# Hybrid decoder trunk on one core: output weights loaded into the place of their low halves, half of them split in the sample stage, loads by readiness, no products with the zero state

## The reference

```python
hn = rmsnorm(x, norm1)
xr, yr, qkv_raw, z, b_raw, a_raw = split(hn @ w_in)          # 512, 512, 1536, 512, 4, 4 columns
xc = causal_conv(xr) + b                                     # 4 taps, history from the state
h = rglru(xc, h0)                                            # a = exp(-8 sigmoid(xc Wa) softplus(-lam)); h = a h + u
out_rg = gelu(yr) * h
q, k, v = silu(causal_conv(qkv_raw)); q, k = l2norm(q) / sqrt(128), l2norm(k)
beta = sigmoid(b_raw); g = -exp(A_log) * softplus(a_raw + dt_bias)
# gated delta rule, per head, in chunks: triangular solve inside a chunk, a 128 x 128 state S between chunks
v_new = u - w @ S;  o = (q e^gc) @ S + qk @ v_new;  S = S * g_last + k_tail^T @ v_new
out_gdn = rmsnorm(o, gdn_norm_w) * silu(z)
x = x + concat(out_rg, out_gdn) @ w_out
hf = rmsnorm(x, norm2); x = x + (silu(hf @ w_gate) * (hf @ w_up)) @ w_down
y = rmsnorm(x, final_norm)                                   # also returned: all conv and recurrent states
```

## Time and profile before

| | us |
|---|---|
| runs before, median of 3 | 1407.17 (1404.64 to 1408.01) |
| the profiled execution's own time | 1404.84 |
| its span, first to last instruction | 1403.1 |
| PE busy | 1359.4 |
| first block: end of the last projection on PE | 367.14 |
| sample stage: from there to the first output product | 57.5 |

### The profile page before, as it was taken

How to read it: one execution, slowest core, us unless ns; L and a number is a source line. 1 busy time by engine, 2 the same in 40 slices (tenths; PEclk the granted TensorE clock), 3 DMA queues, 4 the chain that set the end, 5 groups by cost and what they waited for, 6 DMA issues and landing times.

```text
span 1403.1 us, 19430 instructions
## 1 busy us (share of the span) xinstructions
PE 1359.4 (97%) x7764; PEld 1256.6 (90%) x7764; DVE 632.9 (45%) x923; ACT 382.3 (27%) x766; POOL 153.1 (11%) x225
## 2 busy tenths in 40 slices
PE   6999999999789999999999999999999999999997
PEld 5889999999658888889999999998989898989896
DVE  6446646468345556543423333333342424242427
ACT  6457653323232223222121202020202020202013
POOL 4032034330021322200000000000000000000001
PEclk9999999999769999999999999999999999999999
DMA  6111122644854433344010101010101010100003
GB/s 207 55 50 49 60 75 96 197 130 157 235 163 128 136 113 119 107 178 160 30 61 30 60 30 60 30 60 30 60 30 60 30 60 30 60 30 30 0 0 127
DMA packets 77330, 116.52 MB, mean 83 GB/s; under 512 B 18912, under 2 KB 52640, under 8 KB 77280
## 3 DMA queue, kind: packets, MB, share of 16 engines
q1 hardware_dynamic: 77280, 115.84, 24.7%
HBM read 88.04 MB, written 27.78 MB: 83 GB/s over the span
## 4 chain that ended last, share of the span: by engine, by line
PE 54%; DVE 1%; issue 0%; ACT 0%; POOLq 0%; POOL 0%; ACTq 0%
PE bank L88 18%; PE bank L89 18%; PE bank L87 18%; PE bank L2198 1%; DVE acc L2306 1%; PE bank L2199 0%; PE bank L2196 0%; DVE gu_first_raw L2264 0%; DVE gu_raw L2264 0%; ACT gu_raw L2248 0%; DVE acc L2312 0%; DVE dn_raw L2310 0%; POOLq L2122 0%; POOL fstat L2325 0%; ACTq L2122 0%
## 5 line engine op out<-in xcount | busy, mean ns | idle before, releaser
L87 PE MATMUL bank<-ht_hi,w_hi 128*128 128x364 f32 (+1 forms) x576 | 195.7, 340 | 0.6 <-issue 0.6
L2276 DVE TENSOR_TENSOR hf<-sg,bank 128x364 f32<-128x364 f32 (+1 forms) x66 | 35.1, 532 | 344.0 <-PE bank L89 344.0
L88 PE MATMUL bank<-ht_lo,w_hi 128*128 128x364 f32 (+1 forms) x576 | 189.2, 328 | 0.0
L89 PE MATMUL bank<-ht_hi,w_lo 128*128 128x364 f32 (+1 forms) x576 | 188.9, 328 | 0.0
L87 PE MATMUL bank<-ht_hi,gu_first_hi 128*128 128x364 f32 (+1 forms) x528 | 174.1, 330 | 2.0 <-PEq L173 2.0
L89 PE MATMUL bank<-ht_hi,gu_first_lo 128*128 128x364 f32 (+1 forms) x528 | 174.1, 330 | 0.0
L88 PE MATMUL bank<-ht_lo,gu_first_hi 128*128 128x364 f32 (+1 forms) x528 | 174.1, 330 | 0.0
L88 PE MATMUL bank<-ht_lo,gu_hi 128*128 128x364 f32 (+1 forms) x528 | 172.9, 327 | 0.0
L89 PE MATMUL bank<-ht_hi,gu_lo 128*128 128x364 f32 (+1 forms) x528 | 172.6, 327 | 0.0
L87 PE MATMUL bank<-ht_hi,gu_hi 128*128 128x364 f32 (+1 forms) x528 | 172.3, 326 | 0.0
L2306 DVE TENSOR_TENSOR acc<-acc,bank 128x512 f32<-128x512 f32 x198 | 132.6, 685 | 85.6 <-PE bank L89 85.6
(11 more groups left out here) (287 smaller groups left out, 2154.7 us busy)
## 6 DMA issues: line engine op xcount, KB each, us to landing
w_raw<-in_w_in SPq DMA_DIRECT2D x24, 512.0 KB, 4.4
dn_raw<-in_w_down SPq DMA_DIRECT2D x22, 512.0 KB, 4.3
scratch_qkv<-cb_y SPq DMA_DIRECT2D x12, 512.0 KB, 2.7
gu_first_raw<-in_w_gate SPq DMA_DIRECT2D x11, 512.0 KB, 3.6
gu_first_raw<-in_w_up SPq DMA_DIRECT2D x11, 512.0 KB, 4.4
gu_raw<-in_w_gate SPq DMA_DIRECT2D x11, 512.0 KB, 3.6
gu_raw<-in_w_up SPq DMA_DIRECT2D x11, 512.0 KB, 4.4
xin<-in_x SPq DMA_DIRECT2D x8, 512.0 KB, 5.1
```

Of the source, the lines that this page charges most:

```text
L87: pe.matmul(out, w_hi, x_hi, start=start, stop=False)
L88: pe.matmul(out, w_hi, x_lo, start=False, stop=False)
L89: return pe.matmul(out, w_lo, x_hi, start=False, stop=stop)
L2276: eng.tensor_tensor(hf[b][:, 0:m], sg[b][:, 0:m], psum[2 * b + 1][:, 0:m], ALU.mult).then_inc(hf_done, 1)
```

## The change

- `wo_raw` becomes one table of eight tiles in the place of `wo_lo`; the low half overwrites its own raw tile. The loads need no free buffer any more: four are issued in step 8 behind `acomp`, four behind the state stores at the end of step 11.
- ScalarE and VectorE split four of the eight tiles before the first z tiles, the other four in the second block, among the sample stage's work; the last z tiles have no split ahead of their output.
- SP's order: keys ahead of the Gram stores in steps 5 and 6; the first two states ahead of the solved systems; tables ahead of `ts`; keys of chunk 0 ahead of the last two states and of the last two z stores.
- ScalarE, pair 1: sigmoid, relu and abs behind the second tanh, the two short exponentials behind the large one; the masks are scaled at the end of pair 2 (16) and in pair 3 (20).
- Chunk 1: `key_state` and `query_state` are left out; the right side becomes a copy and the old part of the output a fill with zero.

```diff
     wo_hi = B("wo_hi", [P, KT, D], F32R)
+    wo_raw = Plan(nc, B.at)("wo_raw", [P, KT, D])
     wo_lo = B("wo_lo", [P, KT, D], F32R)
...
+        def load_wo(u):
+            for n in range(2):
+                f = wo_tile(u, n)
+                eng.dma_start(wo_raw[:, f, :], i["w_out"][f]).then_inc(wo_in[u // 2], 16)
...
                 c = 2 * (t - 5)
-                store_pre(c)
-                store_pre(c + 1)
                 if t <= 6:
                     eng.wait_ge(gram, c + 2)
                     load_k(c + 4)
                     load_k(c + 5)
+                store_pre(c)
+                store_pre(c + 1)
             if t == 8:
                 for q in range(2):
                     eng.wait_ge(pre_out[q], 96 * NC // 2)
                 eng.dma_start(acomp[:, :, :], scratch["a"].rearrange("c h b j i -> (c h b) j i")).then_inc(a_in, 16)
+                for u in range(2):
+                    load_wo(u)
...

+        for u in (2, 3):
+            load_wo(u)
         for s in range(2):
-            load_wo(0, s)
             load_w(TZ + s, s)
         store_z(0, 0)
+        store_z(0, 1)
+        eng.wait_ge(w_hi_done, TZ + H)
+        eng.wait_ge(w_lo_done, TZ + H)
+        for h in range(2):
+            eng.dma_start(states[h], i["state_S"][h]).then_inc(ss_pre, 16)
         eng.wait_ge(sol, SOL)
         eng.dma_start(scratch["d"].rearrange("c h b j i -> (c h b) j i"), xt[:, :, :]).then_inc(d_out, 16)
         eng.wait_ge(sol_turned, 1)
@@ -467,33 +475,25 @@
                       xt_turned[:, :, :]).then_inc(d_out, 16)
         eng.wait_ge(sol8, SOL8)
         eng.dma_start(scratch["d8"].rearrange("h b j i -> (h b) j i"), xt8[:, :, :]).then_inc(d8_out, 16)
-        store_z(0, 1)
-        load_wo(1, 0)
+        eng.wait_ge(d_out, 32)
+        eng.wait_ge(cb_conv, 4 * QKV)
+        for name, table in (("d", d_all), ("dt", d_turned)):
+            eng.dma_start(table[:, :, :, :].rearrange("p c h i -> p (c h) i"),
+                          scratch[name].rearrange("c h b j i -> (b j) (c h) i")).then_inc(d_ld, 16)
         eng.wait_ge(d8_out, 16)
         eng.wait_ge(ts_zero, 1)
         for b in range(NS):
             at = slice(b * LS, (b + 1) * LS)
             eng.dma_start(ts[at, :, at], scratch["d8"][:, b].rearrange("h j i -> j h i")).then_inc(ts_in, 16)
-        eng.wait_ge(d_out, 32)
-        eng.wait_ge(cb_conv, 4 * QKV)
-        for name, table in (("d", d_all), ("dt", d_turned)):
-            eng.dma_start(table[:, :, :, :].rearrange("p c h i -> p (c h) i"),
-                          scratch[name].rearrange("c h b j i -> (b j) (c h) i")).then_inc(d_ld, 16)
-        load_wo(1, 1)
-        eng.wait_ge(w_hi_done, TZ + H)
-        eng.wait_ge(w_lo_done, TZ + H)
-        for h in range(2):
-            eng.dma_start(states[h], i["state_S"][h]).then_inc(ss_pre, 16)
-        store_z(1, 0)
-        eng.wait_ge(ss_pre, 32)
-        eng.wait_ge(proj, 3 * (TZ + 3))
-        for h in (2, 3):
-            eng.dma_start(states[h], i["state_S"][h]).then_inc(ss_pre, 16)
         for s in range(2):
             eng.wait_ge(cb_out[s], 16 * PAIRS)
         eng.wait_ge(proj, 3 * (TZ + 3) + 1)
         eng.dma_start(kq_all[:, :, 0:P], chunk_of(scratch["qkv"][0:2 * H], 0)).then_inc(kq_ld, 16)
         eng.dma_start(ue_all[:, :, 0:P], scratch["ue"][0].rearrange("p (w n) -> p w n", n=P)).then_inc(kq_ld, 16)
+        eng.wait_ge(ss_pre, 32)
+        for h in (2, 3):
+            eng.dma_start(states[h], i["state_S"][h]).then_inc(ss_pre, 16)
+        store_z(1, 0)
         store_z(1, 1)
...
         def gate_exponents():

             x, e, relu = (sp[:, m, 0:MT * H] for m in (0, 1, 5))
+            eng.wait_ge(exp_done, 2)
+            eng.activation(e, e, ACT.Exp, scale=-1.0)
+            eng.activation(alog[:, 0:H], alog[:, 0:H], ACT.Exp).then_inc(exp_done, 1)
+
+        def gate_arguments():
+
+            x, e, relu = (sp[:, m, 0:MT * H] for m in (0, 1, 5))
             eng.wait_ge(g_step, G_ARG)
             eng.activation(relu, x, ACT.Relu)
             eng.activation(e, x, ACT.Abs).then_inc(exp_done, 1)
-            eng.wait_ge(exp_done, 2)
-            eng.activation(e, e, ACT.Exp, scale=-1.0)
-            eng.activation(alog[:, 0:H], alog[:, 0:H], ACT.Exp).then_inc(exp_done, 1)
-            eng.activation(beta[:, :, :], graw[:, :, 0:H], ACT.Sigmoid)
...
-            if j >= 2:
-                gate_rows_below(*((0, 12), (20, 32))[j - 2])
+            if j == 3:
+                gate_rows_below(16, 28)
             if j >= 2:
...
@@ -777,12 +780,10 @@
                 e = min(a + m, SEQ)
                 eng.wait_ge(proj, at_proj(j, 1, n))
                 eng.activation(rb_gy[j % 2][:, a:e], bank(1, n)[:, 0:e - a], ACT.Gelu_apprx_tanh)
-                if j >= 2 and n == 1:
-                    gate_rows_below(*((12, 20), (32, MT * H))[j - 2])
+                if j == 3 and n == 1:
+                    gate_rows_below(28, MT * H)
             eng.activation(sample_rows(rb_gy[j % 2])[:, :, 0:LS], by_sample(sample_bank(1)),
                            ACT.Gelu_apprx_tanh).then_inc(evac_done, 1)
-            if isinstance(j, int) and j == 1:
-                gate_exponents()
             split_next(2 * j + 1, 1, j + 2)

             for n, (a, m) in enumerate(GATE_GROUPS):
@@ -795,9 +796,16 @@
             eng.wait_ge(rg_tanh, 6 * j + 6)
             eng.activation(rb_t[:, 0:WC], rb_r[:, 0:WC], ACT.Tanh, scale=rg_now[:, 2:3],
                            bias=rg_now[:, 2:3]).then_inc(rg_t, 1)
+            if j == 1:
+                eng.activation(beta[:, :, :], graw[:, :, 0:H], ACT.Sigmoid)
+                gate_arguments()
             eng.wait_ge(rg_t, j + 1)
             eng.activation(rb_r[:, 0:WC], rb_r[:, 0:WC], ACT.Exp, scale=rg_now[:, 3:4], bias=rg_now[:, 3:4])
+            if j == 1:
+                gate_exponents()
             eng.activation(rb_sq[:, 0:WC], rb_t[:, 0:WC], ACT.Sqrt, scale=0.25).then_inc(rg_sq, 1)
+            if j == 2:
+                gate_rows_below(0, 16)

...
-        def z(j, prefetch):
+        def z(j):
             for s in range(2):
-                for n in range(2):
-                    eng.wait_ge(wo_in[n], 16 * (2 * j + s + 1))
-                    if j == 0:
-                        for q in range(2):
-                            eng.wait_ge(pre_out[q], 96 * NC // 2)
-                    if j == 1:
-                        eng.wait_ge(d_out, 32)
-                        eng.wait_ge(d8_out, 16)
-                    eng.activation(wo_hi[:, wo_tile(j, s, n), :], wo_raw[n][:, :],
-                                   ACT.Copy).then_inc(wo_hi_done, 1)
                 if j == 0:
+                    for n in range(2):
+                        eng.wait_ge(wo_in[0], 64)
+                        f = wo_tile(s, n)
+                        eng.activation(wo_hi[:, f, :], wo_raw[:, f, :], ACT.Copy).then_inc(wo_hi_done, 1)
                     eng.wait_ge(cb_out[s], 16 * PAIRS)
                 eng.wait_ge(z_out[s], 16 * j)
                 for n, (a, m) in enumerate(GROUPS):
@@ -885,11 +887,11 @@
                     eng.activation(cb_y[s][:, a:e], bank(s, n)[:, 0:e - a], ACT.Silu)
                 eng.activation(samp_z[:, bass.ds(2 * j + s, 1), :].squeeze(1), sample_bank(s),
                                ACT.Silu).then_inc(evac_done, 1)
-                if prefetch:
-                    split_next(TZ + 2 * j + s, s, TZ // 2 + j + 2)
-
-        z(0, True)
-        z(1, False)
+                if j == 0:
+                    split_next(TZ + s, s, TZ // 2 + 2)
+
+        z(0)
+        z(1)
...
+        for s in range(2):
+            for n in range(2):
+                f = wo_tile(s, n)
+                eng.wait_ge(wo_hi_done, 2 * s + n + 1)
+                eng.tensor_tensor(wo_lo[:, f, :], wo_raw[:, f, :], f32(wo_hi[:, f, :]),
+                                  ALU.subtract).then_inc(wo_lo_done, 1)
...
         eng.dma_start(normw[:, :], i["norm2"]).then_inc(m_["n2_ld"], 16)
-        eng.wait_ge(wo_lo_done, KT)
         eng.dma_start(rg_in[:, :, :], chunk_of(scratch["rg"], 0)).then_inc(m_["rg_ld"], 16)
...
-            if t == 1:
-                eng.wait_ge(m_["o_done"], 1)
...
+            if t == 1:
+                eng.wait_ge(m_["sq_q"], 1)
...
                         eng.wait_ge(m_["s_done"], 1 + H)
+                        eng.wait_ge(wo_lo_done, KT)
...
-            key_state(t)
+            if t >= 2:
+                key_state(t)
...
-            query_state(t)
+            if t >= 2:
+                query_state(t)
             state_change(t)
...
+        def wo_high(u):
+            eng.wait_ge(wo_in[1], 64)
+            for n in range(2):
+                f = wo_tile(u, n)
+                eng.activation(wo_hi[:, f, :], wo_raw[:, f, :], ACT.Copy).then_inc(wo_hi_done, 1)
+
         eng.wait_ge(st_out, 48)
         eng.wait_ge(z_out[0], 16 * H // 2)
         square_q(0)
+        eng.wait_ge(d_out, 32)
+        eng.wait_ge(d8_out, 16)
+        wo_high(2)
```

(50 more changed lines are left out.)

10 lines of the change are left out of this document (3 added, 7 removed).

## The result

The changed kernel takes 1412.60 us (median of 6 runs, 1411.64 to 1414.04) against 1405.91 for the kernel before in runs on the same chip: a ratio of 1.0047, interval 1.0028 to 1.0066. The change costs 6.7 us. The time lies inside my range, but it is 2.6 us above my forecast, and past the 0.3% up to which I had called it no change (nearly all of the interval lies beyond). The profiled execution has a span of 1410.9 us, 7.8 more than the one before.

The account below looks back on a forecast made before the run. TensorE (PE), busy 97% of the span, was taken to bound the kernel. The terms 7.4 + 8.8 - 10.2 - 3.1 = +2.9 us, on the median 1407.17, gave 1410 us; its own range 1405 to 1415, the whole range 1399 to 1421.

Parts of the forecast that it names:

- (a): Gate exponents moved: PE's 2.70 us wait before tile 4 goes, but tile 6 starts late; +7.4 us.
- rival one: Before tile 6, GpSimd's gate chain with the history copy takes 20.0 us again; 3.7 us more, 1413.8; chance 0.25.
- (b): Reordered loads: PE's 2.8 us for keys go, but tile 19's weights come late; +8.8 us.
- Rival two: Loads cheaper, stores not later: the loads' cost around tile 19 falls to 4.3 + 2.2, time 1407.8; chance 0.20.
- (c): Sample stage after the last projection's end (E): hole gone, solve at E+21.2; -10.2 us, bounds -7.6 and -14.
- Rival three: Sample stage keeps 2.4 GHz throughout once the hole is gone; 1403 us, faster; chance 0.15.
- (d): First prompt step: two groups of eight products with the zero state go; -3.1 us, bounds -2.1 and -3.1.
- my three holes: PE's idle times: 2.70 us before tile 4's gate products, 2.8 us for keys, 9.56 us after the last weight tile.

Follow-up runs that it names:

- e3: Changed kernel with the output weight loads moved behind the weight loads they stood ahead of; 1400.74 us, ratio 0.9975 to the kernel before.
- e7: Changed kernel with output weight loads behind the weight loads and stores again ahead of the key loads; 1398.24 us, ratio 0.9952 to the kernel before.
- e5: Changed kernel with the eight small `ts` loads moved behind the z stores in SP's queue; 1409.75 us, ratio 1.0026 to the kernel before.
- e6: Changed kernel with ScalarE's last four output weight splits and VectorE's low halves ahead of the wait for z stores; 1411.48 us, ratio 1.0037.
- e8: Changed kernel with history copy first, output weight loads behind the weights, small loads last and splits early; 1388.33 us, ratio 0.9873.
- e4: Kernel before with only the products with the zero state left out in the first prompt step; 1402.59 us, ratio 0.9985.
- e9: Changed kernel with history copy first, output weight loads behind weights, small loads last, splits early, stores ahead of key loads; 1384.92 us, ratio 0.9854.
- e1: Changed kernel with ScalarE's gate exponents, sigmoid and gate row copies back where they stood before; 1404.29 us, ratio 0.9994 to the kernel before.
- e2: Changed kernel with GpSimd's copy of tile pair 2's history rows ahead of the chain of gate instructions; 1402.16 us, ratio 0.9977.

## Why the prediction was nearly right, and where it was not

Most of the mechanisms were the ones I named; the sum was 4.9 us short on the profiled executions. That the time came only 2.6 us above the forecast is in part luck: I had added my 2.9 us to 1407.17, and the kernel before had 1405.91 beside the changed one; by these medians the change costs 6.7 us. Another 1.6 us, at the end of the span, were a gain that no part of the change made. By the steps of the sum:

**(a), forecast +7.4, measured +9.0** (9.5 less the 0.5 us ahead of it). ScalarE, GpSimd and VectorE in changed, against the earlier trace rows:

```profile
98.63 1.28 ACT L800 ACT_TABLE_LOAD   x1
...
103.06 0.19 ACT L735 ACTIVATE alog<-alog 128x4 f32<-128x4 f32 x1
```
```profile
103.83 6.14 POOL L1140 TENSOR_TENSOR sp<-sp,expo 128x36 f32<-128x36 f32 x1
110.05 1.51 POOL L1141 TENSOR_TENSOR sp<-sp 128x36 f32<-128x36 f32 x1
...
119.34 0.20 POOL L1164 COPY rb_x<-hist_rg 128x24 f32<-128x24 f32 x1
```
```profile
105.80 1.32 DVE L999 SCALAR_TENSOR_TENSOR rb_sq<-rb_r,rb_sq 128x1112 f32<-128x1112 f32 x1 [7.20 <-ACT rb_sq L806]
...
109.05 2.48 DVE L1005 TENSOR_TENSOR_SCAN rb_h<-rb_r,rb_xc 128x1112 f32<-128x1112 f32 x1
119.74 0.17 DVE L984 COPY rg_now<-rg_calc 128x4 f32<-128x4 f32 x1 [8.21 <-POOL rb_x L1164]
```

The chain with the copy took 16.1 us where I took 16.3, so rival one (20.0 us) falls. But it began 1.3 us later than I said: the tanh came at 97.29 for my 97.11, and I had counted one table load between tanh and the exponentials, where the sigmoid needed its own, 1.28 us. The Trainium skill's page "ScalarE: Activation LUTs", section "Table sets: the hidden batching unit", lists tanh in sigmoid's table set too; a tanh run from that set would need no load before the sigmoid. Here the sigmoid right behind a tanh has one, and none stands between pair 1's gelu rows and that tanh, so the tanh ran from the set loaded for gelu. VectorE's recurrence ran its usual 1.32 us at 105.80 inside the power instruction; the rule of the Trainium skill's page "SBUF — State Buffer", section "Who interferes with whom", again does not show there, while the multiplication behind it took 1.51 us instead of 0.24 and ended with VectorE's scan, as the rule would have it. Tile 6 started at 126.57. Two small slips of mine are in the rest: from my own 101.9 and 16.3 the copy ends at 118.3 and not at 118.1, and I let tile 6 begin 0.1 us behind its weight split, where PE took 0.5. The clock fell, though later than the 2 us behind a hole that I had read: windows of 2 us of changed, against the earlier trace rows:

```profile
120.00:122.00 2.00, 0.00 (x0) 0.93 0.00 0
122.00:124.00 2.00, 0.00 (x0) 0.50 0.00 0
...
130.00:132.00 2.00, 2.00 (x9) 0.51 0.00 0
132.00:134.00 2.00, 2.00 (x10) 1.00 0.00 0
```

PE, idle since 117.54, kept its 2.4 GHz until about 122 and had it back at 132, after 5.4 us of work at 1.2: 2.7 us lost, for my 2.2. (My 4.5 us for the way back were counted from 420.43; PE had been busy since 416.75 there.)

**(b), forecast +8.8, measured +10.0.** In SP's queue the four loads stood ahead of the weights as described, and the weights were taken 17.8 us later than before; 9.5 of that came from (a):

```profile
311.75 1.98 SPq L415 DMA_DIRECT2D wo_raw<-in_w_out  x4
313.82 0.42 SPq L375 DMA_DIRECT2D w_raw<-in_w_in  x1
```
```profile
321.45 1.06 ACT L747 ACTIVATE w_hi<-w_raw 128x1024 fp32r<-128x1024 f32 x1 [15.36 <-DMA w_raw<-in_w_in]
```

So 8.3 of lateness for my 7.1. By the experiments 8.0 us are the four loads with their clock loss (e3) and 2.6 the key order (e7), against 6.7 and 2.1 in my working; 0.6 is gained elsewhere. Rival two (6.5) falls. What I had as a side remark, that PE could wait for VectorE's products instead of keys, is what happened, and so that edit was a pure loss.

**(c), forecast -10.2, measured -7.2: the step that failed.** It reads: "counting on from there I get the last states at E + 9.0 and the z store at E + 10.2". They came at E+12.3 (PE at 399.07) and E+13.8 (ScalarE's squares). The start of the count was right: the tables were issued at E-6.2 for my E-6.6. What went wrong is the issue of the eight small loads, which the change puts behind the tables. The prediction names no price for them; its E + 10.2 comes out if they take what they took ahead of the tables, the first line (E - 6.6, then 3.9 us to issue the tables, 2.75, 1.0 for the keys, 0.8 for the states and 8.1 to the landing make E + 10.0). In changed they took twice that:

```profile
360.84 2.75 SPq L476 DMA_DIRECT2D ts<-scratch_d  x8
```
```profile
380.57 0.37 SPq L481 DMA_DIRECT2D d_all<-scratch_d  x1
...
383.91 5.66 SPq L487 DMA_DIRECT2D ts<-scratch_d  x8
...
390.73 1.14 SPq L495 DMA_DIRECT2D s_state<-in_state_S  x2
391.91 1.15 SPq L459 DMA_DIRECT2D scratch_z<-cb_y  x2
```
```profile
400.50 0.27 ACT L1688 ACTIVATE mp<-bank 64x128 f32<-64x128 f32 x1 [13.04 <-DMA scratch_z<-cb_y]
```

That difference, 2.9 us, is nearly the 3.0 us by which (c) fell short, and e5 bears it out: without the eight loads ahead of the states, E to the solve is 20.8 us, 10.6 less than before the change. The result lies past my bound of -7.6, since I had bounded the landing of the z store by its own past latency and not the issue ahead of it. The rest of the count held: ScalarE's copy ended 7.7 us after its squares began (I had 8.3), and the splits cost 1.3 us of their 4 behind PE's products (e6; I had 2).

Rival three falls, but not for the reason that I gave against it. I had put the low clock down to PE's waits behind E. In changed the clock fell at about 391.4, while PE ran the state products without a gap, 2 us before its wait for the last states began at 393.38. In e8 PE has no wait there at all, and the clock falls among the same products and is back only at about 388, beside the solve. Windows of changed and of e8:

```profile
390.00:392.00 2.00, 2.00 (x18) 0.84 0.46 132
392.00:394.00 2.00, 1.38 (x7) 0.50 1.08 309
```
```profile
376.00:378.00 2.00, 2.00 (x18) 0.89 0.89 304
378.00:380.00 2.00, 2.00 (x11) 0.50 1.06 276
```

So taking the holes away does not keep the sample stage at 2.4 GHz; why the clock falls in these products, no run here shows.

**(d), forecast -3.1, measured -3.0** in changed; alone (e4) between 0 and 4.2. That it agrees to 0.1 us is luck: in the ten profiled executions without these products the stretch takes 29.0 to 31.2 us, 1.4 to 3.6 less than before, with the fall of the clock at different places in it. It stays the least certain by itself.

**The rest, -1.6**, is no part of the change (next section but one). I had no term for it, as I called PE gapless outside my three holes. The table of waits of the kernel before shows more: this hole of 2.0 us, 3.4 us for VectorE's states in the sample stage, and 13.9 us at the start.

Three of my signs did not come as stated: the hole before tile 19 was 5.60 us and not 8 or more, though its weights came 8.3 us late; PE did wait behind E, 5.69 us for the last states, where I had no hole before ScalarE's copy; and the solve came at E+24.3 and not at E+21. (The upper end of my range adds up to 1420.1 from its terms, not to 1421.)

The losses (a) and (b) were together 2.8 us larger and the gain (c) 3.0 us smaller than I had them; both went the same way, and that took the time from inside the 0.3% to outside.

## What to carry to other kernels

Moving an instruction to a place where its own engine is idle says nothing about who reads its result: follow the result's consumer's whole queue, since here one copy that needed none of the gate work stood behind it and cost more than the removed wait gave. In a DMA queue, put what the dense engine needs next first, and re-measure the issue time of each step in its new place, because it depends on what is in the queue ahead. A change that "comes out even" in such a kernel may be several true gains under a few misplaced lines; taking its parts one at a time found almost 2% in it (e9 against changed: 0.9854 and 1.0047).

## What the hardware showed that I had not expected

A hole of the same length, at the same place of the same code, sometimes costs the clock and sometimes not. Between the attention part and the next stage PE stands still for 2.00 us in every execution, with the same work before and behind. The 4 us behind the hole, first in the kernel before, then in changed (length, PE's busy time, granted clock, DMA share, GB/s):

```profile
615.86:619.86 4.00, 3.97 (x15) 0.57 0.77 243
```
```profile
625.29:629.29 4.00, 3.97 (x24) 1.00 0.77 266
```

Of the eleven profiled executions five lost the clock there (before, e1, e4, e8, e9) and six kept it; from the state change to the end the first take 971.7 to 971.9 us, the others 970.2 to 970.3. So a hole of 2 us is worth 1.6 us more or less, which is also the size of the smallest effects above. Waits at the key products show the same: behind 1.71 us at 281.18 changed lost the clock, while e2 (1.70) and e8 (1.86) kept it there. What decides it I did not test.

The issue time on SP's queue is not a constant of an instruction: the first load behind the two tables took about 3 us longer in both orders (5.66 us for `ts` where it took 2.75 ahead of them, and in e5 3.49 us for a key load that took 0.38 in changed).
